# A two-layer hybrid backbone in fp32: the down projections by seven half products, with h in DRAM during the pair phases

## The reference, cut to what matters

```python
def swiglu(h, w_gu, w_down):
    gt, up = jnp.split(h @ w_gu, 2, axis=-1)
    return (jax.nn.silu(gt) * up) @ w_down

def short_conv_mixer(h, w_in, w_conv, w_out):
    bg, cg, xv = jnp.split(h @ w_in, 3, axis=-1)
    return (bg * dwconv(cg * xv, w_conv, SC_PAD)) @ w_out

h = h + g1 * y
h = h + g2 * swiglu(modulate(rmsnorm(h, norm2_g[l]), sh2, sc2), ffn_w_gu[l], ffn_w_down[l])
...
return rmsnorm(h, final_g)
```

## Time and profile before

| | |
|---|---|
| time, median of 3 runs | 2291.73 us (2290.82 to 2292.48) |
| span of the profiled execution | 2288.6 us |
| TensorE (PE) busy | 2234.8 us, 98% |
| VectorE (DVE) busy | 1484.0 us, 65% |
| ScalarE (ACT) busy | 840.3 us, 37% |
| GpSimd (POOL) busy | 1143.8 us, 50% |
| mean TensorE clock granted | 0.995 of full |
| DMA | 282.95 MB, 124 GB/s mean |

### The profile page before, as it was taken

How to read it: one execution, slowest core, us unless ns; L and a number is a source line. 1 busy time by engine, 2 the same in 40 slices (tenths; PEclk the granted TensorE clock), 3 DMA queues, 4 the chain that set the end, 5 groups by cost and what they waited for, 6 DMA issues and landing times.

```text
span 2288.6 us, 27308 instructions
## 1 busy us (share of the span) xinstructions
PE 2234.8 (98%) x10246; PEld 1822.6 (80%) x10246; DVE 1484.0 (65%) x1897; ACT 840.3 (37%) x1396; POOL 1143.8 (50%) x726
## 2 busy tenths in 40 slices
PE   8999999999899999999999999999899999999998
PEld 3788887878688888888888778888688888888886
DVE  5677856854876555558777987665965555555553
ACT  4555546853523332331213522233533333332212
POOL 3323304788455555565434345574365555564340
PEclk9999999999999999999999999999999999999999
DMA  9756568734132222257662122260132222242321
GB/s 332 223 159 175 159 177 205 163 131 134 42 101 83 83 83 83 83 192 258 207 208 78 51 74 74 74 215 2 60 102 90 83 83 83 84 151 90 111 83 74
DMA packets 296942, 282.95 MB, mean 124 GB/s; under 512 B 64783, under 2 KB 242155, under 8 KB 296299
## 3 DMA queue, kind: packets, MB, share of 16 engines
q1 hardware_dynamic: 258747, 257.61, 36.4%
q10 hardware_dynamic: 37488, 21.50, 3.3%
q0 software_dynamic: 576, 2.10, 0.2%
HBM read 226.36 MB, written 57.16 MB: 124 GB/s over the span
## 4 chain that ended last, share of the span: by engine, by line
PE 85%; DVE 6%; DMA 2%; ACT 2%; issue 2%; POOL 1%; SPq 0%; ACTq 0%; DVEq 0%; POOLq 0%
PE bank L1102 27%; PE bank L1104 26%; PE bank L1103 26%; PE bank L1191 1%; DMA q_spill<-qk_raw 1%; PE bank L1332 1%; DVE act_lo L2138 1%; DVE act_hi L2138 1%; PE bank L1357 1%; PE bank L1145 1%; PE bank L1316 1%; PE bank L1358 0%; DVE probs L2519 0%; DVE x_rms L2130 0%; DMA k_lo<-k_spill 0%
## 5 line engine op out<-in xcount | busy, mean ns | idle before, releaser
L2057 DVE SCALAR_TENSOR_TENSOR h<-bank,mods,h 128x512 f32<-128x512 f32 x384 | 287.4, 750 | 260.4 <-PE bank L1104 255.3
L1063 POOL TENSOR_TENSOR slot_lo<-pair_raw,slot_hi 128x512 fp32r<-128x512 f32 x112 | 169.8, 1516 | 288.0 <-ACT slot_hi L1621 288.0
L1063 POOL TENSOR_TENSOR slot_lo<-t_sum,slot_hi 128x512 fp32r<-128x512 f32 x109 | 164.5, 1531 | 153.4 <-ACT slot_hi L1621 153.4
L1063 POOL TENSOR_TENSOR slot<-pair_raw,slot 128x512 fp32r<-128x512 f32 x144 | 232.2, 1634 | 16.0 <-ACT slot L1621 16.0
L2218 DVE TENSOR_TENSOR bank<-bank,p 128x512 f32<-128x512 f32 x53 | 37.0, 698 | 288.3 <-PE bank L1104 288.2
L1102 PE MATMUL bank<-act_lo,slot_hi 128*128 128x512 f32 x436 | 171.1, 392 | 6.6 <-DVE act_lo L2138 5.9
L1621 ACT CAST slot_hi<-pair_raw 128x512 fp32r<-128x512 f32 x112 | 69.0, 616 | 294.4 <-DMA pair_raw<-in_ffn_w_gu 243.6
L1102 PE MATMUL bank<-a,slot_hi 128*128 128x512 f32 x436 | 171.5, 393 | 2.8 <-ACT p L1630 0.9
L1104 PE MATMUL bank<-a,slot_hi 128*128 128x512 f32 x436 | 170.5, 391 | 0.0
L1103 PE MATMUL bank<-act_lo,slot_lo 128*128 128x512 f32 x436 | 169.9, 390 | 0.0
L1104 PE MATMUL bank<-act_lo,slot_hi 128*128 128x512 f32 x436 | 169.9, 390 | 0.0
(11 more groups left out here) (329 smaller groups left out, 5975.0 us busy)
## 6 DMA issues: line engine op xcount, KB each, us to landing
pair_raw<-in_ffn_w_gu SPq DMA_DIRECT2D x88, 512.0 KB, 4.6
mod_in_f<-in_mod_w SPq DMA_DIRECT2D x48, 512.0 KB, 3.7
z_spill<-silu_g SPq DMA_DIRECT2D x88, 256.0 KB, 2.6
mod_in_p<-in_mod_w SPq DMA_DIRECT2D x32, 512.0 KB, 4.5
pair_raw<-in_o_w_in SPq DMA_DIRECT2D x24, 512.0 KB, 3.8
raw<-in_e_w_in SPq DMA_DIRECT2D x20, 512.0 KB, 4.4
low_f<-z_spill SPq DMA_DIRECT2D x40, 256.0 KB, 5.1
a_f<-z_spill SPq DMA_DIRECT2D x18, 512.0 KB, 6.2
```

Of the source, the lines that this page charges most:

```text
L1063: nc.gpsimd.tensor_tensor(low, from_, high, ALU.subtract).then_inc(s_wlo, 1)
L2057: V.scalar_tensor_tensor(out=dst, in0=bank[:, b, :], scalar=mods[:, gate, m:m + 1], in1=dst, op0=ALU.mult, op1=ALU.add).then_inc(s_hup, 1)
```

## The change

The down phases take the form of the pair phases. Hidden tiles are taken two by two (even and odd, `kp` is the number of such a couple), the output features in two halves of four tiles, the tokens in two halves. With z's four pieces B11, B12, B21, B22 (z of even or odd tile by token half) and the weight's four A11, A12, A21, A22, seven half products replace the eight:

- VectorE makes four z sums T1 to T4 per couple (`z_sum`), in the place of z itself where it can; the seven pieces B11, B21, B22, T1 to T4 go to DRAM (`z_parts`).
- Weight sums S1 and S3 (GpSimd) and S2 and S4 (VectorE) of the second weight matrix are made during the pair phase (`w_sum`) from `w_part`, and go to DRAM (`w_sums`). The weight is thus read in the pair phase, and its pieces and sums again in the down phase.
- A down phase is 7 x 11 (F0, F1) or 7 x 4 (S) steps (`DOWN` gives weight piece, z piece and banks of each of the seven). A step is one weight piece and one z piece of 128 x 512 by four feature tiles, that is 12 matmuls, with a bank for each tile: banks `XS` = 0, 3, 4, 5 or `YS` = 1, 2, 6, 7. Buffers are a ring of 8 steps; ScalarE makes high parts 5 steps ahead, GpSimd the low part of the weight, VectorE that of z 4 steps ahead (GpSimd both in the first four steps, and in steps 20 to 25 of S). h is updated only at the end of each of the seven: 12 updates after the first, 4 after each other. The last 4 steps (`TAIL`) are made tile by tile: TensorE waits for the operands of all four first.
- VectorE's order in a down phase: at the last step of each product `down_step` (updates, and what of the next norm stands there) comes ahead of the low part of step j + 4; at other steps behind it. The norm of the next stage's first token half is made within the down phase, in S with a loop at step 23.
- `w_part` and the modulation buffers lie where h lies. So h goes to DRAM in quarters (`put_h_aside`) at the beginning of a stage, and is read back, 4 MB, in the second last pair (`bring_h_back`).
- The modulation units: 32 in F0's pair phase (two a pair from pair 4), 8 in S's, 8 in F1's.
- At the end only the lower four features of token tiles 4 to 7 are turned after the last update; the upper ones are turned, squared and gained (ScalarE makes the row) earlier.

```diff
-            def down_work(st):
-                for r in range(ROUND[st] - 2):
-                    for idx in range(16):
-                        update(OUT[st] + 16 * r, idx, gate_of(st), DOWN_BANK[idx % 4])
-                        if st == F0:
-                            mods_here(r, idx)
+            def down_work(st):
+                n, kp = steps_of(st), KP0[st] + KP[st] - 1
...
+                for j in range(n):
+                    updates_first = j % KP[st] == KP[st] - 1
+                    if updates_first:
+                        down_step(st, j)
+                    if j + 4 < n and not low_by_pool(st, j + 4):
+                        down_low(st, j + 4)
...
+                    if not updates_first:
+                        down_step(st, j)
...
+                if st == S and j == 5 * k + 3:
+                    for i in range(4):
+                        scale(n, 2 + i, 2 + i)
+                        add_squares(n + 1, i)
+                    scale(n, 6, 6)
+                    scale(n, 7, 7)
```

The same loop on ScalarE, and TensorE's list:

```diff
+                if st == S and j == 5 * k + 3:
+                    for i in range(4):
+                        first_half(nx, 2 + i)
+                        square(nx, n + 1, i)
...
+                for i in range(n - TAIL):
+                    down_ready(st, i)
+                    for m in range(4):
+                        mm = down_part(st, i, m)
+                    if i % KP[st] < KP[st] - 1:
+                        mm.then_inc(s_step, 1)
+                    down_joint(st, i)
+                for i in range(n - TAIL, n):
+                    down_ready(st, i)
+                for m in range(4):
...
+                    for i in range(n - TAIL, n):
+                        down_part(st, i, m)
```

VectorE ahead of each pair, and SyncE behind the loads of a pair:

```diff
+            def before_pair(st, p):
+
+                if st == S and p % 3 == 0 and p:
+                    dve.wait_ge(s_z1, PAIR0[S] + p)
+                    for c in (T1, T3, T2, T4):
+                        z_sum(KP0[S] + p // 3 - 1, c)
...
+                for k in w_ops(st, p):
+                    if k % 4 in (S2, S4):
+                        w_sum(st, k)
+                for u in mod_units(st, p):
+                    mod_unit(u)
...
+            def aside_work(st, p):
+
+                for k in w_ops(st, p):
+                    store_w(st, k)
+                for r in w_loads(st, p):
+                    load_w(st, r)
+                for u in mod_units(st, p + 1):
+                    load_mod_f(u)
+                if p == PAIRS[st] - 2:
+                    bring_h_back(st)
```

More of the change, by code:

```diff
@@ new lines, in backbone @@
+        B11, B21, B22, T1, T2, T3, T4 = range(7)
+        S1, S3, S2, S4 = range(4)
+        DOWN = (((0, 0), B11, XS, True), (S2, T2, YS, True), ((1, 0), B21, XS, False), (S3, T3, YS, False),
+                ((1, 1), T4, YS, False), (S1, T1, XS, True), (S4, B22, XS, False))
+        UPDATES = (((0, 1), (1, 0), (1, 1)), ((0, 1),), ((0, 0),), ((1, 1),), ((1, 0),), ((1, 1),), ((0, 1),))
+        UPDATED = tuple(4 * sum(len(u) for u in UPDATES[:q]) for q in range(8))
+        TAIL = 4
+        BOTH = 4
@@ new lines, in down_landed, with down_high_at, low_by_pool, down_low_at @@
+        def down_landed(st, i):
+            before = sum((steps_of(k) - i % RING + RING - 1) // RING for k in range(st))
+            return s_land[i % RING], MOD_DONE + 32 * (before + i // RING + 1)
+        def down_high_at(st, i, j):
+            return s_h2, 2 * sum(steps_of(k) for k in range(st)) + 2 * i + j + 1
+        POOL_LOWS = range(5 * KP[S], 6 * KP[S] + 2)
+        def low_by_pool(st, i):
+            return i < BOTH or (st == S and i in POOL_LOWS)
+        def down_low_at(st, i, j):
+            both = sum(low_by_pool(k, n) for k in range(st) for n in range(steps_of(k))) + sum(low_by_pool(st, n) for n in range(i))
+            steps = sum(steps_of(k) for k in range(st)) + i
+            if j == 1 and not low_by_pool(st, i):
+                return s_lz, steps - both + 1
+            return s_l2, steps + both + j + 1
@@ new lines, in down_part @@
+            def down_part(st, i, m):
+                q, r = divmod(i, KP[st])
+                banks, fresh = DOWN[q][2:]
+                if r == 0:
+                    bank_free(st, q, m)
+                w, x = down_operand(i)
+                at_ = slice(m * P, (m + 1) * P)
+                end = r == KP[st] - 1
+                mm = product(bank[:, banks[m], :], (w[0][:, at_], w[1][:, at_]), x[0], x[1], fresh and r == 0, end, not fresh)
+                if end:
+                    mm.then_inc(s_out, 1)
+                return mm
@@ L2299, in pair_work @@
                         c = PAR["short_w"] + j * FT + tile
-                        steps.run(V.scalar_tensor_tensor(out=conv_t[:, tile % 2, :], in0=t_pad[:, j:j + SEQ], scalar=par[:, c:c + 1],
-                                                         in1=conv_t[:, tile % 2, :], op0=ALU.mult, op1=ALU.add))
-                else:
-                    V.tensor_tensor(conv_t[:, 0, two], first, conv_t[:, 0, two], ALU.mult).then_inc(s_z0, 1)
-                    V.tensor_tensor(conv_t[:, 1, two], c22, conv_t[:, 1, two], ALU.mult).then_inc(s_z1, 1)
@@ L2306, in mods_here @@
-            def mods_here(r, idx):
-                for u in mod_units(r, idx):
+                        steps.run(V.scalar_tensor_tensor(out=zt[:, tile % 2, :], in0=t_pad[:, j:j + SEQ], scalar=par[:, c:c + 1],
+                                                         in1=zt[:, tile % 2, :], op0=ALU.mult, op1=ALU.add))
+                else:
+                    V.tensor_tensor(zt[:, 0, two], first, zt[:, 0, two], ALU.mult).then_inc(s_z0, 1)
+                    V.tensor_tensor(zt[:, 1, two], c22, zt[:, 1, two], ALU.mult).then_inc(s_z1, 1)
```

954 lines of the change are left out of this document (572 added, 382 removed).

## The result

The changed kernel takes 2302.46 us (median of 5 runs, 2297.98 to 2305.8) where the kernel before takes 2292.48 beside it: ratio 1.0044, 95% interval 1.0032 to 1.0057. It is slower by 0.44%. The forecast was 2241, so 61 us are to be found.

The account below looks back on a forecast made before the run. TensorE, 98% busy, was taken to bound the kernel by its matmul list. Span 2288.6 - 70.7 + 18.0 + 2.4 + 1.2 - 1.3 = 2238.2, with 3.1 us around it 2241 us against 2291.73; range 2220 to 2259.

Parts of the forecast that it names:

- The matmuls: Down phases of F0, F1 and S: 312 fewer matmuls at 0.2267 us, -70.7 us.
- What a step needs beside TensorE: nothing: Down phases: casts, low parts, updates and DMA fit a 2.72 us step, loads covered by asking 8 steps ahead; no cost.
- The rival in which the two low parts of a step hold each other up: Down steps on VectorE and GpSimd: a step lasts 3.54 us in place of 2.72, 2375 us in all; chance 0.04.
- The stall at S's tail: End of S's down phase: TensorE waits for VectorE's low part behind step 23's updates and four norm rounds, +18.0 us.
- GpSimd gets one weight sum a pair, 1.3 of its 6.1 us: Pair phases: GpSimd's added sum takes 1.3 us of its 6.1 us idle per pair; no cost.
- z sums wait for the store of the piece they overwrite, 2.6 us, issued before VectorE ends the pair: Pair phases: VectorE's z sums wait for a 2.6 us store issued before VectorE ends the pair; no term in the sum.
- VectorE's gap overflows: Pair phases: VectorE's sums take 1.79 us each and exceed its gap by 2.3 us a pair, 2259 us; chance 0.17.
- The longest burst: Down phases, after the first product: 12 updates delay VectorE's low part to 6.8 us, TensorE wants it at 8.2; no cost.
- S's step 3, +1.2: Start of S's down phase: the first product waits for the last couple's B11 in step 3, +1.2 us.
- The end, -1.3: Kernel end: from last update to last row's end 7.0 us in place of 8.25, -1.3 us.
- its first rival: S's down phase: no tail stall, as scales and squares overlap more or the low part is early, 2221 us; chance 0.11.
- the clock behind it: After the stall at S's tail: twelve matmuls at granted clock 0.50 take 5.2 us in place of 2.7, +2.4 us.

Follow-up runs that it names:

- e1: Changed kernel with VectorE's low part for S's tail made ahead of step 23's updates, scalings and squares: 2294.19 us.
- e15: Changed kernel with GpSimd's weight sums behind the pair's seven low parts, VectorE's order as in the changed kernel: 2278.72 us.
- e8: Changed kernel with GpSimd's 52 weight sums on 8 of 512 columns, VectorE's 52 whole: 2278.10 us.
- e12: Changed kernel with GpSimd's weight sums behind the pair's seven low parts and VectorE's behind the modulation units, no work left out: 2276.36 us.
- e2: Changed kernel with all 104 weight sums, GpSimd's and VectorE's, on 8 columns each: 2276.41 us.
- e16: e11 without its store order in S, so B22's store is again behind the next pair's load: 2261.19 us.
- e11: e10 with ScalarE's square ahead of the two modulated copies of its turn in S's step 23: 2249.61 us.
- e6: e1 with the stores of B21 and B22 in S issued ahead of the next pair's load: 2286.05 us.
- e13: Changed kernel with all 104 weight sums on VectorE, none on GpSimd: 2274.90 us.
- e10: e6 with e12's edits, the moved weight sums of both engines: 2256.49 us.
- e7: Changed kernel with seven of eight modulation units on 8 of 1024 columns and their loads cut as well: 2297.34 us.
- e17: e11 with VectorE's updates, scalings and squares again ahead of the low part for S's tail: 2262.98 us.

## Why the prediction was wrong, step by step

**The matmuls: right.** Of 70.7 us, the down phases of F0 and F1 gave what 132 matmuls each promise (29.9 us): 27.7 in F1, and in F0 39.2, of which 9.3 are gaps of the old form, nearly all of it the six totals (12.6 to 3.3). "What a step needs beside TensorE: nothing" held there as well. The rival in which the two low parts of a step hold each other up did not happen: a step takes 2.78 us on average in F0 and 2.82 in F1, with TensorE's own small matmuls between them, for 2.72 forecast and 3.54 by that rival.

**The stall at S's tail: right in place and mechanism, near in size.** 16.64 us measured for 18.0 forecast, the rounds 3.20 for 3.5. What I did not ask is what would be late next: e1 gave back 8.3 us, not 17, and 6 of the difference are the start of F1, which waited on the same list.

**The failed step: "GpSimd gets one weight sum a pair, 1.3 of its 6.1 us", "Nothing".** The gap was read rightly and it is still in the trace. The sums were never in it. In the code each follows a low part whose successors release `pair_raw` and the slots; moved back by 3.5 us, that release made the next load late, and with it the casts, VectorE's sums, and `silu_first`. Price: 23.7 us (e15), all of it in the order of one engine's list, since the same work at the end of the list costs nothing measurable (e15 2278.72, e8 without GpSimd's arithmetic 2278.10; e12 2276.36, e2 without both engines' 2276.41). The price is measured; what each link of the chain adds to it is not. I compared the amount of work with the amount of idle time, where I should have compared the place of the work with the place of the idle time. The amount was wrong too: two of three pairs have two sums and the third none, not one each, and a sum took 1.75 us beside VectorE, not 1.3, so 3.5 us where I had 1.3. Even that is less than the 6.1 us of the gap.

**The second: "z sums wait for the store of the piece they overwrite, 2.6 us, issued before VectorE ends the pair".** That is nearly so in F0 and F1. In S the store of B21 stands behind a load of 512 KB and that load's own wait, and a store took 4.6 us in F0's pairs and not the 2.6 of the earlier trace rows, with 214 GB/s moved in that window where 102 were before. I read the issue order of F0 for all stages. Price: 11.6 us (e16 against e11), and 8.1 by e6 against e1.

**The rival "VectorE's gap overflows" (2259): half right.** Its symptom came true: VectorE's slack fell from 118.8 to 5.7 us in the window of F1. But VectorE's own work was not the cause: with its 52 sums thin the time was 2294, with 52 more on it (e13) 2275. Its list was late because its inputs were, and some of its two-input operations were longer.

**The longest burst, "ready at 6.8, TensorE wants it at 8.2": right in length, wrong in start.** Twelve updates took 7.98 us as forecast (12 x 0.67 = 8.0), but in S they began at 1528.90, behind two low parts that waited for their casts and behind T4 (1.77 us). The low part of step 7 was 4.23 us late.

**The small terms.** S's step 3, +1.2: no distance over 0.35 us between matmuls from 1515.0 to 1533.9, so 0. The end, -1.3: from the last matmul's start to the end of the span 11.8 us before, 11.6 after, so -0.2. The counts of matmuls and of updates (108 on L2261 and 16 of the mixer) came as read.

**The account.** All steps of e11 from the changed kernel, from 2302.5: the weight sums' order 26.1, the store order and the tail together 19.9 (2276.4 to e10's 2256.5), the square 6.9: 2249.6. The forecast without its stall was 2221, its first rival's time. Of the 28.6 us between, the ledger of e11 puts 17.6 in S: S's pairs are 249.8 (before 245.4) and S's down phase 91.7 (before 89.4), so that stage S gets nothing for its 48 fewer matmuls, 10.9 us. Another 9.3 lie in F1 (pairs 439.2, down 215.7). These were not taken apart further. So the 61 us of the forecast's error are the orders (26.1 + 19.9 + 6.9), less the 20.4 that the forecast had for the stall and the clock behind it, and these 28.6, whose cause stays open.

**Open.** How much of the 24 us is lateness alone and how much the longer VectorE operations that go with it: in every run here the two came and went together (the row's median is 1.62 us or more in each kernel with GpSimd's sums in full between the low parts, 0.69 in each other). By the Trainium skill (SBUF — State Buffer, "SBUF: two separate sides") a two-input VectorE operation and a GpSimd one take turns at a port, and the medians above (1616 ns with GpSimd's late list beside it, 692 without) agree with that rule. But the rule alone, applied to the amount of work, would have put a price on e12 too, where none was measurable. Untested is the rival that follows: that the moved sums help because they meet fewer of VectorE's operations, and not because `pair_raw` is released earlier.

## What to carry to other kernels

Work added to an engine with idle time is free only if it stands where the idle time is: look at the instruction behind each added one and ask what that one releases. With several in-order lists, put what others wait for first and sums that nobody wants yet last, ahead of the engine's own wait; here four such moves (GpSimd's sums, the stores, the tail's low part, the square), with no work removed, turned 0.4% slower into 1.9% faster; a fifth, of VectorE's sums, gave nothing by itself. And when a stall is forecast, follow the same list one step beyond it, since what fed the stall feeds the next start as well.

## What the runs showed of the hardware that was not expected

A store of 256 KB took 4.6 us from issue to landing in F0's pairs of the changed kernel, where the same window of the kernel before has 3.5 and its whole trace 2.6. These are rows of DMA issues in that window (KB each, median us to landing), three of the changed kernel, then the store of before and that of e7, which has 7 of 8 modulation loads cut:

```profile
pair_raw<-in_ffn_w_gu SPq DMA_DIRECT2D x38, 512.0 KB, 4.4
mod_in_f<-in_mod_w SPq DMA_DIRECT2D x32, 512.0 KB, 6.6
z_parts<-zt SPq DMA_DIRECT2D x60, 256.0 KB, 4.6
```

```profile
z_spill<-silu_g SPq DMA_DIRECT2D x42, 256.0 KB, 3.5
```

```profile
z_parts<-zt SPq DMA_DIRECT2D x61, 256.0 KB, 4.7
```

In e7 the window moves 183 GB/s in place of 214 and the stores land no sooner, so those loads are not why. What makes them land later than before stays open.

The clock: in the twelve us around the late step 7 TensorE was busy for 7.77 and the granted clock was 0.89, and around e17's stall of 9.92 us it was 0.71, so part of it at the lower of its two levels (1.2 GHz in place of 2.4). In matmul distances the half clock cost 12.9 us in the six phases of the changed kernel and 1.2 in those of the kernel before. The forecast had 2.4 for it, after its one stall. The two windows, of the changed kernel and of e17:

```profile
1528.00:1540.00 12.00, 7.77 (x32) 6.09 (x31) 12.00 (x17) 5.70 (x10) 6.32 (x5) 0.89 1.00 333
```

```profile
1575.00:1590.00 15.00, 5.08 (x15) 3.77 (x14) 9.66 (x14) 9.93 (x18) 9.88 (x8) 0.71 0.19 71
```
